# Expert products with plain f32 operands, read from the raw weight slabs, and a front that loads its modulation slabs in another order

## The reference

```python
def ec_moe(h, w_router, w_gate, w_up, w_down):
    ...
    gates, idx = lax.top_k(aff.T, cap)
    xe = xf[idx]
    hid = jax.nn.silu(jnp.einsum('ecd,edf->ecf', xe, w_gate)) * jnp.einsum('ecd,edf->ecf', xe, w_up)
    ye = jnp.einsum('ecf,efd->ecd', hid, w_down) * gates[..., None].astype(h.dtype)
    ...

def trunk_layer(...):
    mod = jax.nn.silu(cvec) @ w_ada + b_ada
    shift1, scale1, gate1, shift2, scale2, gate2 = [m[..., None, :] for m in jnp.split(mod, 6, axis=-1)]
    h = rms_norm(x, norm1_g) * (1 + scale1) + shift1
    p, q, k, v = project_mixer_inputs(h, w_in, q_norm_g, k_norm_g)
    ...
    h2 = rms_norm(x, norm2_g) * (1 + scale2) + shift2
    x = x + gate2 * ec_moe(h2, w_router, w_gate, w_up, w_down)
```

## Time and profile before

| | us |
|---|---|
| median of 3 runs | 3220.5 (3218.81 to 3221.09) |
| the profiled execution's own time | 3220.08 |
| its span | 3218.5 |
| TensorE busy | 3098.2 (96%) |
| VectorE busy | 2243.9 (70%) |
| ScalarE busy | 1608.6 (50%) |
| GpSimd busy | 698.7 (22%) |

### The profile page before, as it was taken

How to read it: one execution, slowest core, us unless ns; L and a number is a source line. 1 busy time by engine, 2 the same in 40 slices (tenths; PEclk the granted TensorE clock), 3 DMA queues, 4 the chain that set the end, 5 groups by cost and what they waited for, 6 DMA issues and landing times. The chain is left out here.

```text
span 3218.5 us, 67279 instructions
## 1 busy us (share of the span) xinstructions
PE 3098.2 (96%) x22474; PEld 2803.9 (87%) x22474; DVE 2243.9 (70%) x3959; ACT 1608.6 (50%) x3557; POOL 698.7 (22%) x900
## 2 busy tenths in 40 slices
PE   6989999999999999998999986999999999999999
PEld 4988989998998998997887876999999989998998
DVE  4888878888887887887984556555555555555554
ACT  4556656666665665665762224333333433333332
POOL 2532233333333233332210002111111111111111
PEclk8999999999999999999999997999999999999999
DMA  8654344435335344434335554566655556655664
GB/s 293 239 202 126 121 133 137 127 118 156 118 115 157 118 127 153 130 118 142 127 103 206 205 182 152 187 194 197 196 183 183 183 183 196 197 183 183 196 200 130
DMA packets 341271, 530.91 MB, mean 165 GB/s; under 512 B 29690, under 2 KB 256266, under 8 KB 325770
## 3 DMA queue, kind: packets, MB, share of 16 engines
q1 hardware_dynamic: 331116, 494.53, 47.0%
q0 software_dynamic: 10016, 34.61, 4.3%
HBM read 439.63 MB, written 88.65 MB: 164 GB/s over the span
## 5 line engine op out<-in xcount | busy, mean ns | idle before, releaser
L3039 PE MATMUL ps_gu<-xT,e_w 128*128 128x272 f32 x6144 | 777.9, 288 | 1.6 <-DVE xT L3212 1.6
L3039 PEld LDWEIGHTS ps_gu<-xT,e_w 128*128 128x128 f32 x6144 | 774.1, 188 | 3.3 <-issue 2.0
L3201 DVE TENSOR_TENSOR e_w<-e_raw,e_w 128x2048 fp32r<-128x2048 f32 x190 | 435.1, 2290 | 310.3 <-ACT e_w L3096 310.3
L1197 ACT ACTIVATE e<-ps_s,negm 128x1024 f32<-128x1024 f32 (+2 forms) x416 | 473.9, 1144 | 241.3 <-DVE negm L1598 200.4
L1583 DVE TENSOR_REDUCE mx<-ps_s 128x1 f32<-128x1024 f32 (+3 forms) x428 | 526.6, 1233 | 66.4 <-PE ps_s L834 62.2
L834 PE MATMUL ps_s<-kT,qT 128*128 128x512 f32 (+1 forms) x1920 | 478.2, 386 | 14.1 <-ACT e L1197 12.9
L3096 ACT CAST e_w<-e_raw 128x2048 fp32r<-128x2048 f32 x190 | 361.8, 1904 | 188.6 <-PE ps_d L3021 122.0
L834 PEld LDWEIGHTS ps_s<-kT,qT 128*128 128x128 f32 x1920 | 341.8, 190 | 86.5 <-ACT e L1197 28.5
L908 PE MATMUL ps_m<-w,hT 128*128 128x384 f32 x2040 | 392.0, 340 | 3.9 <-DVE o L1650 3.9
L876 PE MATMUL ps_m<-v,aT 128*128 128x128 f32 x2816 | 369.4, 278 | 1.3 <-ACT aT L1181 1.3
L908 PEld LDWEIGHTS ps_m<-w,hT 128*128 128x128 f32 x2040 | 349.4, 189 | 5.4 <-issue 5.4
(11 more groups left out here) (417 smaller groups left out, 3933.0 us busy)
## 6 DMA issues: line engine op xcount, KB each, us to landing
hT<-hT_d SPq DMA_DIRECT2D x85, 1024.0 KB, 5.4
e_raw<-w_gate SPq DMA_DIRECT2D x64, 1024.0 KB, 5.3
e_raw<-w_up SPq DMA_DIRECT2D x64, 1024.0 KB, 9.0
e_raw<-w_down SPq DMA_DIRECT2D x64, 1024.0 KB, 5.2
tab<-tabs_d SPq DMA_DIRECT2D x85, 256.0 KB, 2.7
hT_d<-hT SPq DMA_DIRECT2D x17, 1024.0 KB, 4.0
w_lent<-w_ada SPq DMA_DIRECT2D x16, 1024.0 KB, 5.5
cat_d<-cat_h SPq DMA_DIRECT2D x102, 128.0 KB, 4.7
```

Source lines behind the costliest of these rows:

```text
L1197: nc.scalar.activation(out, src, ACT.Exp, bias=negm[:, s.par, c:c + 1], scale=HD ** -0.5, accum_out=acc).then_inc(exp_done.sem, 1)
L3039: mm = nc.tensor.matmul(ps_gu[:, 2 * (s % 2) + f, 0:SLOTS], w_view(s, a)[:, k, f * P:f * P + P], xT[:, b, k, :], start=(k == 0 and a + b = ...
L3201: nc.vector.tensor_tensor(w[:, s % RING, 1, :], raw[:, s % RAW, :], w[:, s % RING, 0, :].bitcast(F32), ALU.subtract).then_inc(w_lo, 1)
```

## The change

In the experts all products take plain f32 operands. `e_raw` has six buffers and TensorE reads it directly; the ring `e_w`, the splits of slabs, of `xT`, of the prompt's tokens and of the hidden activations are gone, with the quarters in the selection. SyncE loads a slab when TensorE has read the one six before.

```diff
-RAW, RING, EARLY = 4, 3, 2
+RAW = 6
...
-                    n = SLABS * e + s
-                    wait_positive(sp, w_lo, n - RAW + 1)
+                    wait_read(sp, e, s - RAW)
...
                 for k in ks:
-                    for a, b in ((0, 0), (0, 1), (1, 0)):
-                        for m in ms:
-                            at = CAPP + m * P
-                            mm = nc.tensor.matmul(y_at(half, m), hid[:, b, 4 * part + k, at:at + P], w_view(s, a)[:, k, :],
-                                                  start=(part == 0 and k == 0 and a + b == 0),
-                                                  stop=(part == 1 and k == 3 and a == 1))
+                    for m in ms:
+                        at = CAPP + m * P
+                        mm = nc.tensor.matmul(y_at(half, m), h32[:, 4 * part + k, at:at + P], slab_view(s)[:, k, :],
+                                              start=(part == 0 and k == 0), stop=(part == 1 and k == 3))
...
-                    wait_positive(pe, w_lo, SLABS * e + s + 1)
+                    wait_slab(pe, e, s)
...
-                            for a, b in ((0, 0), (0, 1), (1, 0)):
-                                mm = nc.tensor.matmul(ps_gu[:, 2 * (s % 2) + f, 0:SLOTS],
-                                                      w_view(s, a)[:, k, f * P:f * P + P], xT[:, b, k, :],
-                                                      start=(k == 0 and a + b == 0), stop=(k == KD - 1 and a == 1))
+                            mm = nc.tensor.matmul(ps_gu[:, 2 * (s % 2) + f, 0:SLOTS],
+                                                  slab_view(s)[:, k, f * P:f * P + P], xT[:, k, :],
+                                                  start=(k == 0), stop=(k == KD - 1))
```

```diff
+        SLAB_ORDER = (2, 3, 0, 1)
...
-            for n in range(4):
-                load_slab(n)
+            load_slab(0, slice(0, KD), slab_in[0])
...
+            load_slab(1, slice(0, KD), slab_in[1])
+            load_slab(2, slice(0, KD), slab_in[2])
+            load_slab(3, slice(0, KD // 2), slab_in[2])
+            load_slab(3, slice(KD // 2, KD), slab_in[3])
+            sp.wait_ge(slab_in[2], 32)
...
-            for n in range(3):
-                modulation(n)
+            for i in range(2):
+                modulation(i)
             pe.wait_ge(picked, 3)
-            pe.wait_ge(mod_done, 2)
-            spread_rows(1)
+            for half in range(2):
+                pe.wait_ge(a_row, half + 1)
+                spread_rows(0, half)
+            modulation(2)
+            pe.wait_ge(mod_done, 3)
+            spread_rows(1, 0)
             modulation(3)
-            pe.wait_ge(a_row, 2)
-            spread_rows(0)
             turn_rows(0)
+            for n in range(4):
+                spread_prompt(n)
```

More of the change, by code:

```diff
@@ L325, in stage_heads, with spread_at, prompt_at @@
         qT_dram = nc.dram_tensor("qT_d", (2, NS, P, 2 * P), F32).ap()
+        def spread_at(j, half):
+            return (ps_t[:, half, :], ps_s[:, 512 * half:512 * half + 512])[j]
+        def prompt_at(n):
+            return ps_t[:, n - 1, :] if n in (1, 2) else ps_m[:]
         def wo_slice(n):
@@ L957, in modulation, with spread_rows, spread_last @@
                         mm = nc.tensor.matmul(ps_s[32 * j:32 * j + 32, 512 * n:512 * n + 512], scT32[:, k, :],
-                                              slabs[n][:, k, :], start=(m == 0), stop=(m == 1))
+                                              slabs[i][:, k, :], start=(m == 0), stop=(m == 1))
                 mm.then_inc(ada_done, 1)
[L961 to L967, removed]
+            def spread_rows(j, half):
+                src = (g1row, mod)[j][:, half * 512:half * 512 + 512]
+                nc.tensor.matmul(spread_at(j, half), picker[:, 0, :], src, start=True, stop=True).then_inc(rows_ready, 1)
+            def spread_last():
+                pe.wait_ge(mod_done, 4)
+                spread_rows(1, 1)
             def spread_prompt(n):
@@ L1274, in copy_prompt, with high_rows @@
                 act.wait_ge(rows_p_ready, n + 1)
-                nc.scalar.copy(rows_p[:, j, half * 512:half * 512 + 512], ps_m[:]).then_inc(rows_p_copied, 1)
-            def high_rows(t):
+                nc.scalar.copy(rows_p[:, j, half * 512:half * 512 + 512], prompt_at(n)).then_inc(rows_p_copied, 1)
+            def high_rows(t, halves=range(2)):
                 if t >= 2:
@@ L1280, in high_rows @@
                     qkv_ready.wait(act, Slot(0, t - 1))
-                for half in range(2):
+                for half in halves:
                     act.wait_ge(xT_ready, 2 * t + half + 1)
@@ L1942, in _ @@
-            for t in range(2):
-                means(t)
+            for i in range(2):
+                mod_rows(i)
+                half = slice(512 * i, 512 * i + 512)
+                dve.wait_ge(g1_in, 16)
+                dve.wait_ge(mod_done, i + 1)
+                nc.vector.tensor_tensor(g1row[:, half], mod[:, D + 512 * i:D + 512 * i + 512], g1row[:, half],
+                                        ALU.mult).then_inc(a_row, 1)
+            means(0)
+            scale_first()
+            mod_rows(2)
@@ L2659, in _ @@
                                         ).then_inc(h2p_made, 1)
-            for n in range(2):
-                pool.wait_ge(bound_made, 7 + n)
-                low_piece(n)
-            low_piece(2)
             pool.wait_ge(same_done, 1)
@@ L3019, in down_prompt @@
                     for n in range(4):
-                        slab = raw[:, (8 + 2 * part + n // 2) % RAW, :].rearrange("p (k n) -> p k n", n=512)
+                        slab = slab_view(8 + 2 * part + n // 2)
                         mm = nc.tensor.matmul(ps_d[32 * n:32 * n + CAPP, 2, 0:256], h32[:, 4 * part + k, 0:CAPP],
@@ L3071, in _ @@
                 turn(0, p)
[L3072 removed]
+            pe.wait_ge(xTp_done, PAIRS)
             run_experts(pe, body)
[L3075 to L3082 removed]
         @block.scalar
         def _(act):
[L3086 to L3096 removed]
@@ L3133, in _ @@
+                if more:
+                    turned(e + 1, 0)
+                    place_prompt(e + 1)
+                    for d in range(1, PAIRS):
+                        turned(e + 1, d)
             for p in range(PAIRS):
@@ L3239, in body @@
                         result(e, 0)
-                        if more:
-                            turned(e + 1, s - 8)
-                    split(e, s + 2, more)
-                    if s == 11:
                         result_prompt(e)
@@ L3272, in _ @@
             read_list(0)
-            dve.wait_ge(w_hi, 2)
-            nc.vector.tensor_tensor(w[:, 1, 1, :], raw[:, 1, :], w[:, 1, 0, :].bitcast(F32), ALU.subtract).then_inc(w_lo, 1)
-            for p in range(PAIRS):
-                picked(p)
-            for p in range(PAIRS):
-                turned(0, p)
             dve.wait_ge(gate2_in, 32)
```

310 lines of the change are left out of this document (130 added, 180 removed).

## The result

| | us | against before |
|---|---|---|
| before, median of 3 runs | 3220.5 (3218.81 to 3221.09) | |
| after, median of 3 runs | 3462.8 (3460.58 to 3464.29) | ratio 1.0752 [1.0737, 1.0766] |
| span before, after | 3218.5, 3461.1 | +242.6 |

The account below looks back on a forecast made before the run. The prediction took TensorE's own time, mainly the experts' gate, up and down products, as the bound. It summed 3220.1 + 252 (experts) - 4 (hand-over) - 5 (front) = 3463 us, range 3440 to 3522.

Parts of the forecast that it names:

- Plain f32 is two instructions of two passes: Experts' products: four passes instead of three, 0.230 us per gate/up instruction and 0.428 per down; +252 us.
- No slab is late: Experts: six buffers give each slab five slabs of about 7.3 us to land, so TensorE never waits; no cost.
- At most 9.0: Experts' loads: a slab lands at most 9.0 us after its issue, taken from the median of the slower kind.
- Hand-over -4: Selection to experts: removed subtractions and last low half let experts start sooner; -4 us, bounds -1 and -6.
- The second reading: Hand-over: the gather need not be slowed by VectorE's subtraction if it only reads few indices; term then -2 us.
- Front -5: Before and in the first tiles: earlier first projection and spreads moved ahead of all tiles; -5 us, bounds 0 and -10.
- Its first half: Front: first projection near 49 instead of 52.06, taking the head's low pieces as they come; 2.6 us gained.
- The second half: Front: three prompt-row spreads leave the busy tiles for TensorE's idle time, 0.86 us each; 2.6 us more gained.
- Weight loads come into view: Rival, experts: plain f32 weight loads not hidden behind columns, 0.12 us per instruction, +614; 4077 us; 3 in 100.
- One instruction for each product: Rival, experts: plain products take two passes for three, one instruction each; 2772 us, faster; 3 in 100.
- The excess stays: Rival, experts: the old form's 12 and 21 ns excess per instruction remains, +309; 3520 us; 14 in 100.
- Late slab or clock: Rival, experts: a late slab, or granted clock 0.95 for 1.00 costing some 70 us (3535); 4 in 100.

Follow-up runs that it names:

- e8: The changed kernel with two of eight steps of gate and up and one of four of down, all slabs still loaded; 2653.7 us.
- e6: The changed kernel with one more VectorE subtraction of two raw slabs beside the first gather; 3466.8 us, ratio 1.0761.
- e2: e1 with the load of the fourth tile of x issued ahead of the small constants; 3215.6 us, 0.9981 against before.
- e1: The changed kernel's new front and order of loads with the experts as before; 3217.4 us, 0.9994 against before.
- e5: The changed kernel with 64 of 272 columns in seven of eight steps of each gate and up product; 3041.4 us.

## Why the prediction was right

**Plain f32 is two instructions of two passes: right.** 4096 and 1024 instructions, 0.2292 and 0.430 us, where 0.428 was read from a run of two instructions and 0.230 from the line through that and a run of four. By the records that makes 938.8 + 440.3 = 1379.1 us for 1128.6, +250.5. An expert grew by 15.6 us, from 76.9 to 92.5. The stage grew by 247.6: sixteen times 15.6 is 249.6, and what stands beside the sixteen became 2.0 us shorter (1485.4 - 16 x 92.5 = 5.4 for 1237.8 - 16 x 76.9 = 7.4). These 2.0 are the granted clock: the first 240 products of the kernel before took 1.9 us more than the same run in a later expert, at 0.81. The sum had taken one clock for the whole stage. It was 4 us too much of 252, about 2 by its prices and 2 by that clock.

**No slab is late: right.** TensorE has not one wait for a slab, and an up slab lands in 5.1 us, for 9.0 before; why it is sooner was not tried. "At most 9.0" was a wrong reading: it is the median of the up slabs, and the latest slab before landed after 12.0 us. Against the 36 us that five slabs give, this changes nothing. e8 shows how far away the limit is: 41.9 us of transfers under 92.5 of products.

**Hand-over -4: right, -4.5 measured, and each part was at its place.** The gather with its landing gave 2.2 (e6 gives it back with one instruction), L2614 1.0, and the last low half 0.6 where 0.9 was estimated. Another 0.5 is luck: the turns ran at a granted clock of 1.00 for 0.77. The second reading was wrong: the sentence of the Trainium skill, "SBUF — State Buffer", section "Who interferes with whom", that a VectorE instruction with two SBUF inputs blocks a GpSimd instruction that reads SBUF, does hold for the gather, which I had taken for a reader of few indices. e6 agrees with that sentence, 3.27 us for 1.21, and the -2 that I had drawn from it was my own reading of what a gather reads, not what the page says.

**Front -5: too much.** This is the step that failed. Its first half came true, but not by its reason: the first projection began at 47.0, before the 49.4 that I had called a floor, because the floor was wrong. VectorE's low pieces were done at 41.64 + 4.11 = 45.75, all of them ahead of the projection, so taking them one by one gained nothing there. VectorE came to them 3.7 us sooner: before, the scaling and shifting of tiles 0 and 1 stood in front of them from 39.2 us on (L1692, L1695); now tile 0's is done by 35.0 and tile 1's begins at 37.0 (L1730, L1740). The moved spreads can be seen too: from tile 0's projection to tile 1's it is 8.21 us for 9.84, 1.6 less, which is two spreads of 0.86. The second half, that a lead at tile 0 is still there after tile 2, was not followed. At tile 2 it met two things that the sum had left out: a tile of x, issued behind small loads (1.9 to 3.2 us, e2), and the lambda steps now between the tiles. By the trace the front gave 1.3 us, by e1's median 3.3, with an interval that also holds no gain at all. The bounds of 0 and -10 held it.

**Why the total is so close.** By the traces it was 4 too much for the experts, 4 too much gain in the front, half a microsecond in the hand-over, and 0.8 from an unchanged stretch: 3463 is right to 0.2 us by cancelling, and that is luck. The steps themselves are good to some 4 us each, of which the granted clock in short stretches is a part that the sum could not know.

**The rivals.** *Weight loads come into view*: no. e5 gives 0.111 us for what may be the load; my upper bound of 0.12 was near, and the mistake of that rival was only to add it to the columns instead of holding it against them. The rule on fast loads of the Trainium skill, "TensorE: Matmul & The Clock Gate", section "Weight-path perf modes — Fast Weight Load (FWL) and DoubleRow", did not show as a longer load against the split form: 190 ns for plain f32, 188 for float32r. That comparison cannot test the rule, though, since float32r has four bytes too; the bf16 loads of the list (L3013) are 96 ns, half as long. *One instruction for each product*: no, 4096. *The excess stays*: no, 272 columns have 2.5 ns over two bare passes (0.2267), where the split form had 12. *Late slab or clock*: no; the clock is 1.00.

## What to carry to other kernels

Work on engines that hide behind another is not worth a microsecond of that other: this change took 521 us from VectorE and 394 from ScalarE, and cost 248 on TensorE. Price a form of matmul from start to start in a run of them at the same clock, even a run of two that stands elsewhere in the trace; that gave 0.430 and 0.2292 us to half a percent. Before two traces are compared over a few microseconds, look at the granted clock on both sides: here it made 1.3 us at the first tile, 1.3 to 1.7 in the turns and 2.0 in the first expert. A lead at the start of a pipeline must be followed to the first stage in which another input is late, and its DMA may stand behind small loads that nobody waits for.

## What the runs showed of the hardware

- An indirect gather on GpSimd takes 0.97 us by itself, 1.21 at its first, and 3.27 where it begins 0.10 us into a VectorE subtraction of two SBUF operands that takes 2.29 (e6). A scatter that begins 1.14 us into one takes 2.58 for 1.55, and one that is 0.75 us under way when it begins takes 1.59 as ever; a gather beside a subtraction with one operand in PSUM takes 0.96 (the kernel before).
- A plain f32 instruction with 64 columns takes 0.111 us from start to start at full clock (e5), one of bf16 with 10 columns 0.025.
- Two passes of plain f32 have almost no excess (2.5 ns at 272 columns, 3 at 512), one pass of float32r has 12 and 21 ns. Why the single pass has it is open.
- A 512 KB load behind fourteen small loads of constants was issued 7.2 us later than ahead of them, and landed 10.6 us after its issue, with the DMA share at 0.24, where two such loads ahead of them landed in 6.5 and 6.8 (e2). Why it takes longer to land was not tried.
- With the slabs, gathers and scatters of an expert the DMA engines were full at 347 GB/s (e8).
- The stretch from 201 us to the router, TensorE's work the same in all, took 1742.0 us before, 1742.8 after, 1738.6 in e1 and 1744.4 in e2. So a difference of a few microseconds is read at the marks on either side of a change, not at the end of the span.
